# Prompt attention in another order and with more buffers: the key search of mixer B spread over mixer C, mixer B computed last

## What is computed

```
# A, 4 heads: stick breaking
z = q k^T * scale; log_keep = where(causal, log_sigmoid(-z), 0)
a = where(causal, exp(log_sigmoid(z) + cumsum_after(log_keep)), 0); o = a v
# B, 6 heads: each query keeps the top k = min(256, L/4) = 128 keys by a token index score
vals, idx = top_k(where(causal, score, -inf), k)
p = masked_softmax(q k_sel^T * scale + bias); o = p v_sel
# C, 6 heads: three softmax branches, each with a gate
o = g0 * o_cmp (blocks of 32 keys) + g1 * o_slc (blocks, here all) + g2 * o_win (window 512)
masked_softmax: e / maximum(sum(e), 1e-30)
# the output of each head is multiplied by silu of its gate path
```

## Time and profile before

| | us |
|---|---|
| median of three runs (lowest and highest) | 2874.64 (2871.42 to 2877.35) |
| the profiled execution's own time | 2872.88 |
| its span, first to last instruction | 2871.1 |
| `prompt_attention` in it, first to last busy instruction | 2342.5 to 2629.3 |

### The profile page before, as it was taken

One profiled execution on the slowest core, in us unless ns is written; L12 is line 12 of the kernel. 1 busy time (PEld: TensorE's weight loads), 2 busy tenths in 40 slices (PEclk: granted clock), 3 DMA queues, 4 the chain that ended last, 5 costly groups with the idle time before them and its releaser, 6 DMA issues. The chain is left out here.

```text
span 2871.1 us, 45368 instructions
## 1 busy us (share of the span) xinstructions
PE 2357.2 (82%) x16097; PEld 1786.6 (62%) x16097; DVE 1051.7 (37%) x1869; ACT 760.9 (27%) x1706; POOL 485.2 (17%) x335
## 2 busy tenths in 40 slices
PE   5999999999967989966588687884996544787996
PEld 3888888888867989963355344442554323665885
DVE  5101111101011222223488476664332279556213
ACT  3000000000011222210344345542553353344010
POOL 6433333333240000000000000000000000233431
PEclk7999999999979999979799799997998665898998
DMA  5333232332468786514899799995996630002223
GB/s 177 119 104 110 100 121 90 112 112 80 168 164 257 240 234 213 185 27 93 265 356 342 263 386 386 379 376 158 365 379 236 217 88 0 1 1 96 88 81 117
DMA packets 344412, 522.93 MB, mean 182 GB/s; under 512 B 67501, under 2 KB 150846, under 8 KB 341902
## 3 DMA queue, kind: packets, MB, share of 16 engines
q1 hardware_dynamic: 309722, 483.10, 50.3%
q10 hardware_dynamic: 31792, 32.05, 3.7%
q0 software_dynamic: 2704, 5.33, 0.6%
HBM read 498.09 MB, written 44.00 MB: 189 GB/s over the span
## 5 line engine op out<-in xcount | busy, mean ns | idle before, releaser
L461 PE MATMUL proj_acc<-proj_w_hi,h_hi 128*128 128x512 f32 (+1 forms) x960 | 369.9, 385 | 8.5 <-POOL proj_w_lo L430 8.5
L462 PE MATMUL proj_acc<-proj_w_hi,h_lo 128*128 128x512 f32 (+1 forms) x960 | 369.9, 385 | 0.0
L463 PE MATMUL proj_acc<-proj_w_lo,h_hi 128*128 128x512 f32 (+1 forms) x960 | 369.4, 385 | 0.0
L430 POOL TENSOR_TENSOR proj_w_lo<-w_in,proj_w_hi 128x2048 fp32r<-128x2048 f32 (+1 forms) x60 | 272.8, 4548 | 458.8 <-DVE proj_w_hi L399 458.8
L754 PE MATMUL cmp_hp<-cmp_xT,cmp_w 128*128 128x128 f32 x2048 | 253.1, 278 | 12.2 <-DVE cmp_xT L785 12.2
L399 DVE CAST proj_w_hi<-w_in 128x2048 fp32r<-128x2048 f32 (+1 forms) x60 | 81.1, 1356 | 465.9 <-PE proj_acc L454 463.1
L754 PEld LDWEIGHTS cmp_hp<-cmp_xT,cmp_w 128*128 128x128 f32 x2048 | 241.1, 194 | 16.3 <-DVE cmp_xT L785 15.9
L1250 PE MATMUL sb_tp<-kept_consts,sb_k_rows 128*128 128x128 f32 x1024 | 169.5, 315 | 64.1 <-DMA sb_k_rows<-in_cache_sb_kv_dram 47.9
L485 ACT COPY proj_out<-proj_acc 128x512 f32<-128x512 f32 (+1 forms) x60 | 34.7, 579 | 697.0 <-PE proj_acc L463 697.0
L1250 PEld LDWEIGHTS sb_tp<-kept_consts,sb_k_rows 128*128 128x128 f32 x1024 | 127.0, 158 | 136.8 <-ACT sb_kT L1390 63.0
L461 PEld LDWEIGHTS proj_acc<-proj_w_hi,h_hi 128*128 128x128 f32 x960 | 180.7, 188 | 44.3 <-issue 8.8
(11 more groups left out here) (407 smaller groups left out, 3583.6 us busy)
## 6 DMA issues: line engine op xcount, KB each, us to landing
cmp_rows<-in_cache_nsa_kv_dram SPq DMA_DIRECT2D x512, 128.0 KB, 2.4
slc_rows<-in_cache_nsa_kv_dram SPq DMA_DIRECT2D x256, 256.0 KB, 5.0
sb_k_rows<-in_cache_sb_kv_dram SPq DMA_DIRECT2D x256, 256.0 KB, 6.0
sb_v_rows<-in_cache_sb_kv_dram SPq DMA_DIRECT2D x256, 256.0 KB, 7.2
dsa_rows<-in_cache_dsa_kv_dram SPq DMA_DIRECT2D x256, 256.0 KB, 4.8
w_in<-in_w_in_dram SPq DMA_DIRECT2D x56, 1024.0 KB, 5.0
fin_w<-in_w_out_dram SPq DMA_DIRECT2D x32, 512.0 KB
proj<-proj_out ACTq DMA_DIRECT2D x14, 1024.0 KB, 4.3
```

Of the source, the lines that this page charges most:

```text
L430: pool.tensor_tensor(w_lo[q][:, :, 0:width], w[q][:, :, 0:width], w_hi[q][:, :, 0:width], ALU.subtract).then_inc(lo_made, 1)
L461: pe.matmul(to, h_hi[:, kk, r], w_hi[q][:, k, 0:width], start=(kk == 0), stop=False)
L462: pe.matmul(to, h_lo[:, kk, r], w_hi[q][:, k, 0:width], start=False, stop=False)
L463: last = pe.matmul(to, h_hi[:, kk, r], w_lo[q][:, k, 0:width], start=False, stop=(kk == KT_IN - 1))
```

## The change

The units of mixer B go to the end of the list: 16 "stick", 72 of mixer C, 24 "dsa". The search is no longer done in the first 16 rounds, six instructions a round: its 96 instructions are spread over rounds 0 to 83, one in most rounds and two in every seventh, and each waits only for the one two places before it. Eighteen of them fall in the 16 rounds of mixer A and 78 in those of mixer C. The padding maxima of a head are taken four at a time, those of the first head in rounds 0 to 3 and those of the others in the first four rounds of the head before.

The pipeline gets deeper: PE turns unit u-3 and multiplies unit u-5, and the copies are made for unit u-3. There are three banks `sc` and `tp`, three `pT`, six `L` and two `soft`; ACT does the three softening steps of unit u before the second exponential of unit u-1. The floor of 1e-30 stays only in "cmp" units of tile 0. The gate is no longer multiplied on DVE: POOL takes it as the second factor of the same instruction.

```diff
@@ -2010,28 +2010,35 @@
     n_stick = len(units)
     for h in range(6):
         for i in range(4):
-            units.append(Unit("dsa", 4 + h, i, 4 + h, 4 + h // 3, 4 + h // 3, h, None, True, True))
-    for h in range(6):
-        for i in range(4):
             units.append(Unit("slc", 10 + h, i, 10 + h, 6 + h // 3, 6 + h // 3, 6 + h, 6 + h, True, False))
             units.append(Unit("win", 10 + h, i, 10 + h, 8 + h // 3, 8 + h // 3, 6 + h, 12 + h, False, False))
             units.append(Unit("cmp", 10 + h, i, 10 + h, h // 3, h // 3, 6 + h, h, False, True))
+    n_free = len(units)
+    for h in range(6):
+        for i in range(4):
+            units.append(Unit("dsa", 4 + h, i, 4 + h, 4 + h // 3, 4 + h // 3, h, None, True, True))
     N = len(units)
     for u, x in enumerate(units):
         x.u = u
     outs = [x.u for x in units if x.last and x.tile == 3]
...
+    place = {units[u].out: n for n, u in enumerate(outs)}
+    LB, SB, TB = 6, 3, 3
+    TURN, MUL = 3, 5
...
-        L = [s.sb(f"logits{i}", [P, XW]) for i in range(4)]
-        soft = s.sb("soft", [P, SEQ])
+        L = [s.sb(f"logits{i}", [P, XW]) for i in range(LB)]
+        softs = [s.sb(f"soft{i}", [P, SEQ]) for i in range(2)]
         top8 = s.sb("top8", [P, 3, 8])
-        pT = [s.sb(f"pT{i}", [P, 4, P]) for i in range(2)]
+        pT = [s.sb(f"pT{i}", [P, 4, P]) for i in range(TB)]
...
-        sc = [s.ps(f"sc{i}", [P, SEQ]) for i in range(2)]
-        tp = [s.ps(f"tp{i}", [P, 4, P]) for i in range(2)]
+        sc = [s.ps(f"sc{i}", [P, SEQ]) for i in range(SB)]
+        tp = [s.ps(f"tp{i}", [P, 4, P]) for i in range(TB)]
...
-        assert n_stick >= TOPK_P // 8
+        n_ops = TOPK_P // 8 * 6
+        ops_until = lambda u: min(n_ops, (u + 1) * n_ops // (n_free - 4))
...
             def score(x):
-                if x.u >= 2:
-                    before = units[x.u - 2]
+                if x.u >= SB:
+                    before = units[x.u - SB]
                     if before.kind == "stick":
-                        pe.wait_ge(added, x.u - 1)
+                        pe.wait_ge(added, before.u + 1)
...
             def turn(x):
                 if x.kind == "stick":
                     pe.wait_ge(ready_stick, x.u + 1)
                 else:
                     pe.wait_ge(ready, x.u - n_stick + 1)
-                if x.u >= 2:
-                    pe.wait_ge(copied[x.u % 2], x.u // 2)
+                if x.u >= TB:
+                    pe.wait_ge(copied[(x.u - TB) % 2], (x.u - TB) // 2 + 1)
...
-            for u in range(N + 3):
+            pe.wait_ge(cleared, LB)
+            for u in range(N + MUL):
                 if u < N:
                     score(units[u])
-                if 2 <= u < N + 2:
-                    turn(units[u - 2])
-                if u >= 3:
-                    product(units[u - 3])
+                if TURN <= u < N + TURN:
+                    turn(units[u - TURN])
+                if u >= MUL:
+                    product(units[u - MUL])
...
-                pool.tensor_scalar(v, v, rcp[:, x.u:x.u + 1], 1.0, ALU.mult, ALU.mult).then_inc(ready, 1)
+                gate = 1.0 if x.gate is None else kept.pgates[:, x.tile, x.gate:x.gate + 1]
+                pool.tensor_scalar(v, v, rcp[:, x.u:x.u + 1], gate, ALU.mult, ALU.mult).then_inc(ready, 1)
...
-                    if x.u:
-                        act.wait_ge(soft_dve, 4 * x.u)
-                    t = soft[:, 0:x.w]
-                    act.wait_ge(soft_act, chain.step(act.activation(t, sc[x.u % 2][:, 0:x.w], ACT.Abs)))
+                    if x.u >= 2:
+                        act.wait_ge(soft_dve, 4 * x.u - 4)
+                    t = softs[x.u % 2][:, 0:x.w]
...
-            for u in range(N + 3):
+            for u in range(N + TURN):
+                if u < n_stick:
+                    exp(units[u])
                 if 1 <= u <= n_stick:
                     exp_stick(units[u - 1])
-                if u < N:
+                if n_stick <= u < N:
                     exp(units[u])
-                if 2 <= u < N + 2 and u % 2:
-                    copy(act, units[u - 2])
+                if u >= TURN and (u - TURN) % 2:
+                    copy(act, units[u - TURN])
...
-            dve.wait_ge(cleared, 4)
-            for h in range(6):
-                for i in range(4):
-                    chain.step(dve.tensor_reduce(pad_max[:, h, i:i + 1], kept.bias[:, 6 + h, 0:SEQ - i * P], AX.X, ALU.max, negate=True))
+            dve.wait_ge(cleared, LB)
+            pad_step = {}
+            def pad(h, i):
+                pad_step[h, i] = chain.step(dve.tensor_reduce(pad_max[:, h, i:i + 1], kept.bias[:, 6 + h, 0:SEQ - i * P], AX.X, ALU.max, negate=True))
...
-                dve.wait_ge(small, chain.step(dve.tensor_scalar(r, sums[:, x.u:x.u + 1], 1e-30, None, ALU.max)))
-                if x.gate is None:
-                    dve.reciprocal(r, r).then_inc(rcp_ready, 1)
+                total = sums[:, x.u:x.u + 1]
+                if x.kind == "cmp" and x.tile == 0:
+                    dve.wait_ge(small, chain.step(dve.tensor_scalar(r, total, 1e-30, None, ALU.max)))
+                    total = r
+                dve.reciprocal(r, total).then_inc(rcp_ready, 1)
+            def best(n):
+                r, i = divmod(n, 6)
+                if i < 3:
+                    own = kept.score[:, i + 1, 0:(i + 2) * P]
+                    if r:
+                        dve.wait_ge(top_step, n - 2)
+                    dve.max(top8[:, i, :], own).then_inc(top_step, 1)
                 else:
-                    dve.wait_ge(small, chain.step(dve.reciprocal(r, r)))
-                    dve.tensor_tensor(r, r, kept.pgates[:, x.tile, x.gate:x.gate + 1], ALU.mult).then_inc(rcp_ready, 1)
-            def best(r):
-                if r:
-                    dve.wait_ge(top_step, r * 6)
-                for i in range(1, 4):
-                    dve.max(top8[:, i - 1, :], kept.score[:, i, 0:(i + 1) * P]).then_inc(top_step, 1)
-                for i in range(1, 4):
-                    dve.wait_ge(top_step, r * 6 + i)
-                    dve.match_replace(kept.score[:, i, 0:(i + 1) * P], top8[:, i - 1, :], kept.score[:, i, 0:(i + 1) * P], GONE).then_inc(top_step, 1)
-            for u in range(N + 4):
+                    own = kept.score[:, i - 2, 0:(i - 1) * P]
+                    dve.wait_ge(top_step, n - 2)
+                    dve.match_replace(own, top8[:, i - 3, :], own, GONE).then_inc(top_step, 1)
+            for u in range(N + MUL + 1):
                 if u < N:
                     add(units[u])
-                if u < TOPK_P // 8:
-                    best(u)
-                if u == TOPK_P // 8 - 1:
-                    dve.wait_ge(top_step, TOPK_P // 8 * 6)
-                    for i in range(1, 4):
-                        dve.tensor_scalar(kept.dropp[:, i, 0:(i + 1) * P], kept.score[:, i, 0:(i + 1) * P], GONE / 2, NEG, ALU.is_gt, ALU.mult).then_inc(dropped, 1)
                 if 1 <= u <= N:
                     invert(units[u - 1])
-                if 2 <= u < N + 2 and u % 2 == 0:
-                    copy(dve, units[u - 2])
-                if u - 4 in outs:
-                    dve.wait_ge(multiplied, u - 3)
-                    h = units[u - 4].out
-                    to = kept.oT[:, h, :].rearrange("p (m t) -> p m t", m=4)
-                    dve.tensor_tensor(to, to, ov[h % 2][:], ALU.mult).then_inc(out_done, 1)
+                if TURN <= u < N + TURN and (u - TURN) % 2 == 0:
+                    copy(dve, units[u - TURN])
+                if u - MUL - 1 in outs:
+                    dve.wait_ge(multiplied, u - MUL)
+                    x = units[u - MUL - 1]
+                    to = kept.oT[:, x.out, :].rearrange("p (m t) -> p m t", m=4)
+                    dve.tensor_tensor(to, to, ov[place[x.out] % 2][:], ALU.mult).then_inc(out_done, 1)
+                if u < n_free:
+                    for n in range(ops_until(u - 1), ops_until(u)):
+                        best(n)
+                    if u < 4:
+                        pad(0, u)
+                    elif u >= n_stick and (u - n_stick) % 12 < 4 and (u - n_stick) // 12 < 5:
+                        pad((u - n_stick) // 12 + 1, (u - n_stick) % 12)
+                if n_free - 4 <= u < n_free - 1:
+                    i = u - (n_free - 4) + 1
+                    dve.wait_ge(top_step, n_ops)
+                    dve.tensor_scalar(kept.dropp[:, i, 0:(i + 1) * P], kept.score[:, i, 0:(i + 1) * P], GONE / 2, NEG, ALU.is_gt, ALU.mult).then_inc(dropped, 1)
```

More of the change, by code:

```diff
@@ L2066, in score @@
                 if x.kind == "cmp":
-                    pe.matmul(sc[x.u % 2][:, 0:x.blocks], q, kept.cmp_kp[:, x.k, 0:x.blocks], start=True, stop=True).then_inc(scored, 1)
+                    pe.matmul(sc[x.u % SB][:, 0:x.blocks], q, kept.cmp_kp[:, x.k, 0:x.blocks], start=True, stop=True).then_inc(scored, 1)
                     return
@@ L2071, in score @@
                     pe.wait_ge(dropped, 3)
```

(50 more changed lines are left out.)

25 lines of the change are left out of this document (12 added, 13 removed).

## The result

The changed kernel takes 2783.80 us, median of four runs (2777.18 to 2788.54), where the kernel before takes 2873.03 (four runs). The ratio is 0.9684, with a 95% interval of 0.9665 to 0.9703: 3.2% faster, or 89 us. The forecast was 2806 us with a range of 2790 to 2832.

What follows compares the result with a forecast made beforehand. DVE was taken to bound mixer A, and too short a pipeline mixer C, where PE would bind after the change. 7.1 + 37.1 + 19 + 4.2 - 1.3 = 66.1 us less than 2872.9 gave 2806 us, range 2790 to 2832.

Steps and rivals of the forecast that it cites:

- The start: Before DVE's first step of unit 0: 7.1 us less, as the padding maxima ahead of it go; bounds 6.5 and 7.5.
- Mixer A: First 16 units: DVE's sum of 54.7 us plus 1 us for waits, 55.7, or 37.1 us less; bounds 54.7 and 62.
- Mixer C: The 72-unit stage: PE binds, closely followed by DVE; 114 us in all, 19 us less; bounds 101 and 133.
- 5 us of unevenness: In mixer C: an estimated 0.9 us a head, over six heads, added to PE's work for uneven tiles.
- The forecast for that sum: DVE's work in mixer C: 74.5 - 21.6 + 47.6 = 100.5 us; the stage's lower bound, 101, was put near it.
- PE reaches its full clock: Rival, chance 0.22: in mixer C PE's work shrinks to 96 us at best, DVE binds, stage 102, total 2795 us.
- a clock near 1.0 with C at 102: Sign that would show the forecast wrong: PE's granted clock near 1.0 and mixer C lasting 102 us.
- PE must wait for DVE at tile 0: Argument against the full-clock rival: at tile 0 of mixer C DVE has more to do; no size given.
- Mixer B and the end: Last stage 41.5 us, 4.2 less, bounds 39 and 45.7; after the last add 6.5 us, 1.3 more, bounds 5 and 8.
- Mixer C doesn't keep its time: Rival, chance 0.18, claiming it does: added DVE work breaks up PE's work, mixer C stays at 133, total 2826 us.
- All added DVE work shows: Rival, chance 0.04: mixer C gets 26 us longer, total 2852 us, only if PE and DVE can't overlap.
- POOL's second factor: In mixer C's rows: 76 ns each, 5.5 us at most, hidden; rival of POOL as bound, slower than before, chance 0.02.

Runs made afterwards that it cites:

- ring_only: Kernel before with only the deeper pipeline (turn u-3, product u-5, six L, three sc, tp and pT): 2829.61 us, ratio 0.9845.
- no_search_c: Changed kernel without the 78 search instructions of mixer C, so mixer B drops other keys: mixer C 88.9 us, section 187.5 us.
- ring_old: Changed kernel with the pipeline of before (turn u-2, product u-3, four L, two sc, tp and pT): 2826.82 us, ratio 0.9837.
- lag_old: Changed kernel with its banks but the order of before (turn u-2, product u-3): mixer C 133.3 us, section 241.8 us.
- search_only: Kernel before with only the search spread and mixer B put last: 2856.68 us, ratio 0.9933.
- columns_back: Changed kernel with the floor (90 of 96 units) and the gate multiplication back on DVE: 2809.42 us, ratio 0.9773.

## Why the prediction was right in its sign and too small

**The start** was forecast 7.1 us shorter and is 7.2 (10.1 to 2.9). As a gain it is spent, though: with the maxima ahead the whole section is only 1.8 us longer. The sum counted it and the 7.9 us in mixer C separately and so had the account right.

**Mixer A**: 55.7 forecast, 54.4 measured. DVE's sum without waits was 54.7; it is busy for 50.4. The reading that a second `soft` is needed for that is shown by the run without it, 66.5 us.

**Mixer C**: this is the step that failed. The prediction put it as "PE: 108.8, unchanged in number" and added 5 us of unevenness, 114. The number of matmuls was unchanged, and their time was not. A busy time of PE at a granted clock of 0.88 isn't a constant that goes into a sum: it shrinks when the waits go, here to 92.8 us in the changed kernel and 89.8 with the deeper pipeline alone. Nor is busy time times clock its floor, as the prediction had it: 108.8 x 0.88 gives 96, "at best", and both came out below. PE works throughout in the low stretches (3.40 of 3.40 us in the row above) and its idle time falls almost wholly into the upper ones, so the mean over the stretch is too high for its work; how much of the gap that explains is open. Of the 40.6 us by which ring_only shortens mixer C, 19.0 are such work (108.8 to 89.8) and the other 21.6 idle time. Then the bound isn't PE but DVE, and the stage follows DVE's sum: 94.5 us busy in 99.4. The forecast for that sum was 100.5, a second term too large, so 101 stood as a lower bound that the stage went under. With no_search_c DVE is busy for 62.5, so 78 search instructions add 32.0 us to its busy time, 0.41 each, where the sum took 0.495 from a round in mixer A; that is 6.6 us, and the sum is 6.0 too large. The 5 us for uneven tiles happen to be what DVE is idle for, but for another reason: it waits 3.1 us for ACT's sums, not for PE.

That is the rival *PE reaches its full clock*, which foresaw 102 us for the stage and had 0.22. The prediction named its sign, "a clock near 1.0 with C at 102", and it came: 0.98. What spoke against it, that PE must wait for DVE at tile 0, isn't what the trace shows: PE idles for 6.2 of 99.0 us, and its longer waits stand 5 to 10 us behind the first add of a head, at the middle tiles. The rival's 102 was luck in part. It had PE's work at 96 and DVE's at 100.5, each too high, and its total of 2795 us would still have been 11 too high.

**Mixer B and the end**: 41.5 + 6.5 = 48.0 forecast, 41.3 measured. It is the same error, smaller. PE's 38.8 us at 0.96 were taken as a floor, with 39 as the lower bound; it is 35.6 at 1.00. By the adds mixer B takes 35.3 us (2492.8 to 2528.1), about 5.9 a head where it was 7.6, and the end takes 6.0.

The sum of the misses: 0.1 at the start, 1.3 in A, 14.6 in C, 6.7 in B and the end, 22.7 in all. 2806.8 - 22.7 = 2784.1, and 2783.8 was measured.

**The other rivals** fell. Mixer C doesn't keep its time, except with the old order, where ring_old and lag_old show 127.9 and 133.3 us. *All added DVE work shows* exists in part. In search_only, with the old order, mixer C has 143.1 us, 10 more than before, when DVE had got 37.5 us of work more (74.0 to 111.5 between the same adds). With the new order it shows as soon as DVE is the bound: with the one-column steps on DVE in both, mixer C is 92.4 us without search and maxima (ring_only) and 121.9 with them (columns_back), 29.5 us more for 43.5 of DVE's work. POOL's second factor costs 86 ns at 512 columns, where 76 were taken. POOL is busy for 46.3 of 99.0 us in mixer C, so it isn't the bound:

```profile
L2143 POOL TENSOR_SCALAR pa_logits<-pa_logits,pa_rcp,kept_pgates 128x512 f32<-128x512 f32 x12 | 9.3, 778 | 8.3 <-DVE pa_rcp L2251 8.3
...
L2143 POOL TENSOR_SCALAR pa_logits<-pa_logits,pa_rcp 128x512 f32<-128x512 f32 x6 | 4.1, 692 | 2.3 <-DVE pa_rcp L2251 2.3
```

**The parts don't add up**, and that was missing from the argument. The ring alone saves 47.4 us, the search with the new order alone 19.2, 66.6 together; the whole saves 88.8. Taken away last, the ring is worth 37.7 (ring_old), the one-column steps 22.7, the second `soft` 12.1, the spread maxima 1.8. The second `soft` has something to give once the search has left mixer A, as DVE's waits for ACT in search_only show. The one-column steps give 22.5 us in mixer C where DVE is the bound, at least 15 with the search in it and the old order, and at most 2.6 in ring_only. Taken alone out of the kernel before they were not measured.

## What to carry to other kernels

Before PE's busy time goes into a sum, look at the granted clock. Under 1.0, in a stage with waits, part of the busy time goes away with the waits: here 108.8 us at 0.88 became 92.8 and 89.8. Busy time times clock (96 us) tells the direction and isn't a floor. Then look what engine is next, because it may be the bound.

Where two engines of a hand-ordered pipeline wait for each other and neither is full, give the order more lag first. Here a turn one round later and a product two rounds later were worth 26 to 34 us in one stage, and 41 with the banks in a kernel without the search there; the banks beside it gave 2.5. Short steps off an engine are worth what that engine is short of: 22 us where DVE was full, at least 15 where the ring was short and the search was on DVE, under 3 where PE was full. Work that only changes its place on the engine that bounds both places gains next to nothing (1.8 us of 7.5); moving it to an engine with time left gains until the next engine is full.
